# Eight slots for split weights, and norms that start token tile by token tile, in a two-block transformer kernel

## The reference

```python
def first_block(x, ...):                    # two layers
    # layer 0: differential attention (8 heads), layer 1: chunked attention with
    # a relative bias (16 heads); FFN of width 2816
    x = layer_norm(DEEPNORM_ALPHA * x + mix, ...)
    x = layer_norm(DEEPNORM_ALPHA * x + swiglu(x, w_in, w_out), ...)
...
def second_block(x, ...):
    z = rmsnorm(h, pre_mix_g) @ w_in        # then a gMLP and a gated linear attention mixer
    h = h + rmsnorm(concat(a, b) @ w_out, post_mix_g)
    f = rmsnorm(h, pre_ff_g) @ w_ff1
    h = h + rmsnorm(square(relu(f)) @ w_ff2, post_ff_g)
```

## Time and profile before

| | |
|---|---|
| runs | 1957.37, 1959.56, 1962.37 us; median 1959.56 |
| the profiled execution | 1956.62 us, span 1954.9 us, mean granted clock 0.978 |
| TensorE | 1843.4 us busy, 94%, 8392 matmuls |
| DVE, ACT, GpSimd | 938.2, 680.3 and 173.2 us busy |
| weight tiles | 309: 269 split by DVE, 40 by GpSimd |

### The profile page before, as it was taken

How to read it: one execution, slowest core, us unless ns; L and a number is a source line. 1 busy time by engine, 2 the same in 40 slices (tenths; PEclk the granted TensorE clock), 3 DMA queues, 4 the chain that set the end, 5 groups by cost and what they waited for, 6 DMA issues and landing times.

```text
span 1954.9 us, 21070 instructions
## 1 busy us (share of the span) xinstructions
PE 1843.4 (94%) x8392; PEld 1469.8 (75%) x8392; DVE 938.2 (48%) x1524; ACT 680.3 (35%) x1104; POOL 173.2 (9%) x108
## 2 busy tenths in 40 slices
PE   8998888999999899999799999996999879999998
PEld 7766667888888676666688888875877668888886
DVE  3688755333333824555633333357342654344344
ACT  3344432222223334554232222233445443323242
POOL 0322101000000500000200000013000240000000
PEclk9999999999999999999999999998999989999999
DMA  6322113333333432222133333343322333333231
GB/s 219 101 71 84 60 55 88 102 92 101 100 94 115 129 116 84 81 65 64 56 97 97 97 98 97 97 143 101 87 56 63 119 108 107 97 97 97 87 108 54
DMA packets 222744, 184.96 MB, mean 95 GB/s; under 512 B 9220, under 2 KB 178086, under 8 KB 222647
## 3 DMA queue, kind: packets, MB, share of 16 engines
q1 hardware_dynamic: 222646, 183.62, 30.9%
HBM read 181.45 MB, written 7.38 MB: 97 GB/s over the span
## 4 chain that ended last, share of the span: by engine, by line
PE 83%; DVE 13%; ACT 2%; issue 1%; POOL 0%; DMA 0%; SPq 0%; POOLq 0%; DVEq 0%; ACTq 0%
PE ps L472 25%; PE ps L473 24%; PE ps L474 24%; PE ps L759 2%; DVE x L1275 2%; DVE x L1280 2%; PE ps L769 1%; PE ps L719 1%; PE ps L781 1%; PE ps L658 1%; DVE stat L1367 1%; DVE arena L1305 1%; DVE xl L1196 1%; DVE wlo L1188 1%; DVE small L1263 1%
## 5 line engine op out<-in xcount | busy, mean ns | idle before, releaser
L1188 DVE TENSOR_TENSOR wlo<-raw,whi 128x1024 fp32r<-128x1024 f32 x269 | 330.2, 1229 | 489.6 <-ACT whi L924 487.8
L472 PE MATMUL ps<-xh,whi 128*128 128x512 f32 (+1 forms) x1416 | 547.9, 387 | 6.0 <-DVE xl L1196 6.0
L474 PE MATMUL ps<-xh,wlo 128*128 128x512 f32 (+1 forms) x1416 | 535.3, 378 | 0.0
L473 PE MATMUL ps<-xl,whi 128*128 128x512 f32 (+1 forms) x1416 | 535.1, 378 | 0.0
L924 ACT ACTIVATE whi<-raw 128x1024 fp32r<-128x1024 f32 x309 | 324.0, 1053 | 325.8 <-PE ps L474 323.9
L472 PE MATMUL ps<-whi,hh 128*128 128x512 f32 x800 | 319.7, 400 | 14.6 <-POOL wlo L1521 6.3
L472 PEld LDWEIGHTS ps<-xh,whi 128*128 128x128 f32 x1416 | 271.6, 192 | 58.2 <-DVE xl L1196 7.2
L473 PE MATMUL ps<-wlo,hh 128*128 128x512 f32 x800 | 315.0, 394 | 0.0
L474 PE MATMUL ps<-whi,hl 128*128 128x512 f32 x800 | 314.8, 393 | 0.0
L474 PEld LDWEIGHTS ps<-xh,wlo 128*128 128x128 f32 x1416 | 270.5, 191 | 49.0
L473 PEld LDWEIGHTS ps<-xl,whi 128*128 128x128 f32 x1416 | 271.0, 191 | 47.7 <-issue 2.9
(11 more groups left out here) (186 smaller groups left out, 1497.0 us busy)
## 6 DMA issues: line engine op xcount, KB each, us to landing
raw<-in_ffn_w_in SPq DMA_DIRECT2D x88, 512.0 KB, 3.8
raw<-in_w_ff SPq DMA_DIRECT2D x64, 512.0 KB, 3.9
raw<-in_ffn_w_out SPq DMA_DIRECT2D x56, 512.0 KB, 3.8
raw<-in_a_w_qkv SPq DMA_DIRECT2D x24, 512.0 KB, 5.1
raw<-in_w_in SPq DMA_DIRECT2D x20, 512.0 KB, 3.7
raw<-in_kv_w SPq DMA_DIRECT2D x16, 512.0 KB, 3.7
raw<-in_w_out SPq DMA_DIRECT2D x16, 512.0 KB, 3.8
bias_skewed<-bias_rows SPq DMA_DIRECT2D x8, 640.0 KB
```

Source lines behind the costliest of these rows:

```text
L472: e.matmul(o, ah, bh, start=start, stop=False)
L473: e.matmul(o, ah, bl, start=False, stop=False)
L474: return e.matmul(o, al, bh, start=False, stop=stop)
L1188: e.tensor_tensor(self.wlo[:, m % RING, :], self.raw[:, m % RING, :], f32(self.whi[:, m % RING, :]), ALU.subtract).then_inc(s.lo, 1)
```

## The change

- Split weights no longer lie in a ring of four but in slots: SPLIT = 6 always, and EXTRA = 2 more in the arena while attention and mixer don't need that room (`open_extra`, `close_extra`), so eight at every norm. `raw` stays a ring of four. DVE splits every tile.
- The last half ahead of a norm is one run over all its blocks (`runs = [blocks]`), token tile by token tile; `pairs` is gone. The transposes of tiles 0 and 1 stand inside tiles 2 and 3. FFN_GROUPS puts the group of six first, so that the last has four blocks.
- The step `feat` is TensorE's part alone; `xsplit` is that of ACT and DVE. The normalisation is a step `ln` of its own. `waiting` holds `pump` back from token tile 3 on.
- `projections` begins 4 (norms 1 to 3), 5 (norm 4) or 6 jobs (norm 5) on half the tokens, and attention B starts with it too: its values come behind the first four jobs, their second half inside `fill`, and AHEAD_B is 12.
- The mixer makes q0 and q1 within `projections` and interleaves its small steps with the value and gate products; four steps of the product with `w_out_2` (before: two) stand ahead of `squares(3)`. Several arena addresses move, `stat` shrinks, and 1024 bytes are reserved for dynamic DMA.

```diff
-RING = 4
-FFN_GROUPS = [(0, 8), (8, 8), (16, 6)]
+RAW = 4
+SPLIT = 6
+EXTRA = 2
+FFN_GROUPS = [(0, 6), (6, 8), (14, 8)]
 LN_EXP, SQRT, SILU = "natural_log_exp_and_others", "sqrt_and_others", "silu_and_others"
 
 AHEAD_A = 8
 ORDER_A = "- t3 - S0 S1 F0 w F1 - T0 S2 T1 S3 F2 - - - F3 n T2 -".split()
-AHEAD_B = 4
+AHEAD_B = 12
...
-    def pump(self):
-        while self.n_split < len(self.tiles) + RING - 1 and (
-                self.n_split < RING or self.n_split - RING in self.finished):
-            if self.on_pool:
-                self.pool_tiles[self.n_split] = len(self.pool_tiles)
+    def pump(self, most=2):
+
+        while most and self.slots and not self.waiting and self.n_split < len(self.tiles) + SPLIT + EXTRA:
+            slot, free = self.slots.pop(0)
+            self.slot_of.append(slot)
+            self.free_at.append(free)
+            if slot >= SPLIT:
+                self.extra_used[-1][slot] = self.n_split
             self.step("split", self.n_split)
             self.n_split += 1
+            most -= 1
 
     def take(self, *source):
         self.tiles.append(source)
         self.pump()
+        assert self.n_split >= len(self.tiles)
         return len(self.tiles) - 1
 
     def done(self, tile, sem, value):
         self.finished[tile] = (sem, value)
+        if self.slot_of[tile] < SPLIT or self.extra:
+            self.slots.append((self.slot_of[tile], (sem, value)))
         self.pump()
 
-    def settle(self):
-        while self.settling:
-            self.step(*self.settling.pop(0))
+    def open_extra(self, sem, value):
+
+        self.extra = True
+        self.extra_used.append({})
+        self.slots.extend((SPLIT + i, (sem, value)) for i in range(EXTRA))
+
+    def close_extra(self):
+        self.extra = False
+        self.slots = [x for x in self.slots if x[0] < SPLIT]
...
-    def projections(self, wanted, functions):
-        jobs = [self.job(*w) for w in wanted[:3]]
-        self.settle()
-        for job in jobs:
-            self.step("half", job, 0)
-        for norm, t in self.carry:
-            self.feat(norm, t)
-        self.carry = []
+    def projections(self, wanted, functions, norm, n):
+
+        jobs = []
+
+        def half(i):
+            if i < n:
+                jobs.append(self.job(*wanted[i]))
+                self.step("half", jobs[i], 0)
+
+        half(0)
+        if norm < 4:
+            self.feat(norm, 2)
+            self.xsplit(norm, 2)
+            self.step("ln", norm, 3)
+            half(1)
+            half(2)
+            self.feat(norm, 3)
+            self.xsplit(norm, 3)
+        else:
+            self.step("yscale", norm, 2)
+            self.step("ln", norm, 3)
+            self.waiting = False
+            self.pump(1)
+            half(1)
+            half(2)
+            self.feat(norm, 2)
+            self.xsplit(norm, 2)
+            self.step("yscale", norm, 3)
+            self.pump(1)
+            half(3)
+            half(4)
+            self.feat(norm, 3)
+            self.xsplit(norm, 3)
+        self.waiting = False
+        for i in range(len(jobs), n):
+            half(i)
...
+            ends = nh == 1 and norm is not None
+            if ends:
+                runs = [blocks]
+                self.step("table", SQRT)
+            elif nh == 1:
+                runs = [[k] for k in blocks[:-n]] + [blocks[-n:]]
...
+                    if ends and t == 3:
+                        self.waiting = True
...
+                        if ends and norm >= 4 and last and t == 3:
+                            self.feat(norm, 1)
+                            self.xsplit(norm, 1)
+                            self.step("ln", norm, 2)
...
+                        if ends and first and t == 3 and norm >= 4:
+                            self.feat(norm, 0)
+                            self.xsplit(norm, 0)
+                        elif ends and first and t >= 2 and norm < 4:
+                            self.feat(norm, t - 2)
+                            self.xsplit(norm, t - 2)
+                            if t == 3:
+                                self.step("ln", norm, 2)
...
+                            if ends and t < 2:
+                                if norm >= 4 and t == 1:
+                                    self.step("yscale", norm, 0)
+                                self.step("ln", norm, t)
+                            elif ends and t == 2 and norm >= 4:
+                                self.step("yscale", norm, 1)
...
+        self.open_extra("scores", 64)
...
+                self.projections(wanted, SILU, norm - 1, 4)
...
+        self.close_extra()
+        self.projections([(kind, p, w, c + p * 128) for p in range(2)
+                          for kind, w, c in (("q_b", "b_w_q", 0), ("k_b", "kv_w", 0))], LN_EXP, 2, 4)
         values = self.rows("v", ("kv_w", 1024), 0, 8, hh=False)
-        for i in range(32):
-            if i in (6, 9):
-                self.feat(*self.carry.pop(0))
-            if i == 9:
-                self.on_pool = False
-                self.step("table", LN_EXP)
+        out = self.rows("res", ("b_w_o", 0), 0, 8, norm=3)
+        for _ in range(16):
...
+            yield from proj(2)
+            yield from values
+            for p in range(3, 8):
...
+        out = self.rows("w", ("w_out_2", 0), 0, 8, k_first=4, norm=5)
+        for _ in range(4):
+            next(out)
...
-                    w.wait_ge(s.hi, m + 1)
-                    e.tensor_tensor(self.wlo[:, m % RING, :], self.raw[:, m % RING, :],
-                                    f32(self.whi[:, m % RING, :]), ALU.subtract).then_inc(s.lo_pool, 1)
-                    before = self.lo_at[m]
```

More of the change, by code:

```diff
@@ L150, in projections, with rows @@
             self.post(job)
-        for w in wanted[3:]:
+        for w in wanted[n:]:
             self.run(self.quarters(*w))
-    def rows(self, kind, source, row0, nk, k_first=0, ends=False, pairs=False, hh=True, norm=None, group=0):
-        later = []
+    def rows(self, kind, source, row0, nk, k_first=0, grouped=False, hh=True, norm=None, group=0):
         blocks = [(k_first + k) % nk for k in range(0, nk, 2)]
         n = min(3, len(blocks))
[L160 to L165, removed]
+        for nh in range(2):
+            ends = nh == 1 and norm is not None
[4 more added lines that the diff above has]
+                runs = [[k] for k in blocks[:-n]] + [blocks[-n:]]
+            elif grouped:
@@ L166, in rows @@
                 runs = [blocks[:n]] + [[k] for k in blocks[n:]]
             else:
-                runs = [[k] for k in blocks[:-n]] + [blocks[-n:]]
+                runs = [[k] for k in blocks]
             out, taken = {}, {}
             for run in runs:
[L171 to L174, removed]
+                for t in range(4):
+                    if ends and t == 3:
+                        self.waiting = True
@@ L247, in attention_a @@
         self.step("prepare_a")
-        out = self.rows("res", ("a_w_o", 0), 0, 8, ends=True, norm=1)
+        out = self.rows("res", ("a_w_o", 0), 0, 8, norm=1)
         def proj(h):
@@ L330, in fill @@
                 yield
-        self.step("bias", 0)
-        self.step("bias", 1)
-        self.run(proj(0))
         pieces = fill()
@@ L426, in mixer @@
         self.step("load_norm", 5)
-        out = self.rows("w", ("w_out_2", 0), 0, 8, k_first=4, ends=True, pairs=True, norm=5)
-        for h in range(4):
-            self.h[h] = 0
-        next(out)
-        next(out)
+        out = self.rows("w", ("w_out_2", 0), 0, 8, k_first=4, norm=5)
+        for _ in range(4):
+            next(out)
         self.squares(3)
@@ L479, in __init__ @@
     def __init__(self, new):
-        self.raw = [new(f"raw{i}") for i in range(RING)]
+        self.raw = [new(f"raw{i}") for i in range(RAW)]
         self.x = [new(f"x{i}") for i in range(4)]
@@ L665, in tensor @@
                 b = job.bank
-                wh, wl = self.weight(self.whi, job.tile, 8), self.weight(self.wlo, job.tile, 8)
+                wh, wl = self.weight(job.tile, 8)
                 if what == "half":
@@ L1005, in scalar @@
                     e.activation(self.mb[:, t, c], ps[b][:], ACT.Copy).then_inc(s.fb, 1)
-                if r.norm is not None and r.nh == 1:
-                    w.wait_ge(s.eps, 2)
-                    w.wait_ge(s.var, 4 * (r.norm - 1) + t + 1)
-                    e.activation(lsum[:, t:t + 1], mv[:, 2 * t + 1:2 * t + 2], ACT.Sqrt,
-                                 bias=eps6 if r.kind == "w" else eps5).then_inc(s.std, 1)
                 if r.kind == "f" and r.group == 3:
@@ L1021, in scalar @@
                                      scale=1.0 / D).then_inc(s.froot, 1)
+            elif what == "ln":
+                norm, t = arg
+                w.wait_ge(s.eps, 2)
+                w.wait_ge(s.var, 4 * (norm - 1) + t + 1)
+                e.activation(lsum[:, t:t + 1], mv[:, 2 * t + 1:2 * t + 2], ACT.Sqrt,
```

(1 more changed line is left out.)

234 lines of the change are left out of this document (118 added, 116 removed).

## The result

The changed kernel takes 1914.18 us (median of four runs, 1911.62 to 1916.28) against 1959.32 for the kernel before: the ratio is 0.9768, with a 95% interval of 0.975 to 0.9785. It is faster by 45 us. Forecast were 1873 and a range of 1860 to 1897, so the sign is right and half of the gain is missing: 41 us. The profiled execution took 1916.28 us, with a span of 1914.6.

What follows compares the result with a forecast made beforehand. TensorE bounds the kernel, busy 1843.4 of 1954.9 us; 93.2 us of idle and lost clock, less 1.4, 0.4, 3.6, 1.0 and 0.5, give 86.3 gained: 1959.56 - 86.3, forecast 1873 us, range 1860 to 1897.

Steps and rivals of the forecast that it cites:

- Six slots for four in attention A: Attention A: more split slots cost nothing; its 22.5 us of idle stay, give or take 3.
- the likeliest case: Whole kernel: the change works as forecast, 1873 us, own range 1860 to 1882; chance 0.63.
- The norms: Five norms: their 88.6 us of idle and lost clock go, except a 1.4 us stall at norm 4.
- handovers: Whole sum: 0.5 us taken for handovers not exactly as in the timeline.
- The signs named beforehand: No normalisation pass over 0.8 us, DVE split x289, transposes waiting under 3 us in all, clock 1.00 at every norm.
- the rival in which it stays low: Norms: the clock falls as now, 22.7 us stay lost, 1896 us; chance 0.05.
- The rival in which DVE becomes the bound: Norms: four splits in each chain, 24.6 us, and some 10 of clock, 1908 us; chance 0.07.
- Ahead of w_out_2: 1520 to 1540 us: with 24 matmuls instead of 12 on each side of `squares`, 4.6 us become 0.4.
- Attention B: Its start, values' second half under the first two pairs of heads with four banks held: 1 us lost.
- a sign of being wrong: Attention B: idle beyond 2 us in its first two pairs of heads would show the prediction wrong.
- The half jobs: Jobs run as two halves, 23 instead of 12: eleven times 0.33, 3.6 us added.
- the "in part" rival: Norms: small margins open a wait of 2 to 5 us at each, clock whole, 1883 to 1898; chance 0.2.

Runs made afterwards that it cites:

- e1: Changed kernel with split steps emitted at the take of the next weight tile, from attention A only: 1874.67 us, ratio 0.9571.
- e2: Kernel before with its pump bound RING instead of RING - 1, so splits stand where the changed kernel has them: 1989.43 us, ratio 1.0158.
- e6: Changed kernel with split steps at the take of the next tile throughout the whole network: 1868.48 us, ratio 0.954.
- e3: Kernel before with all splits on DVE and none on GpSimd, one line changed: 1920.95 us, ratio 0.9804.
- e9: e5 with `waiting` never set, so splits are not held back at a norm: 1880.06 us, ratio 0.9601.
- e5: Changed kernel with split steps at the take of the next tile in attention A and attention B: 1871.49 us, ratio 0.9556.
- e7: e5 with three half jobs at every norm, 15 jobs in halves for 23: 1891.45 us, ratio 0.9659.
- e4: Changed kernel with `done`, and so the split step, moved behind the job's own `post` step everywhere: 1885.56 us, ratio 0.9624.

## Why the prediction came out 41 us too low

**The step that failed** is one of those costed at nothing: "Six slots for four in attention A, whose TensorE waits for DVE's softmax and not for splits: its 22.5 us stay, give or take 3." They became 45.5, with 16.5 more of clock: 39.5 us. The observation in it was true, TensorE of the kernel before did not wait for splits, and it does not now. It waits for passes that stand behind a split. The prediction asked whether a split is late for its user; the question was what stands behind it in its queue, and it had asked just that of `waiting` at the norms. e1, e2 and e6 show it from three sides: the new kernel without the new place loses the cost, the old kernel with the new place gets it, and with the old place everywhere the changed kernel takes 1868.5, which is inside the likeliest case's own range of 1860 to 1882. No rival had this mechanism in attention A, so the range ended at 1897.

**The norms** were right. 88.6 us were to go but for 1.4; of norms 1 to 3 nothing is left. At norm 4 the idle time is 1.76 where the timeline gave 1.4, and its longest wait is the one worked out, for `xl` (1.6 us); 1.7 of clock come with it that I had not counted; norm 5 has 0.5, as much as the sum allowed for handovers. The four passes of a tile take 750 ns each, so that tile 0 is normalised 5.2 us after its residual add begins, for 5.3 worked out. The signs named beforehand are there: no pass over 0.76 us, 289 splits on DVE, and 0.2 us in all that the transposes wait for DVE. This is DVE's timeline of the changed kernel, norm 3:

```profile
955.63 0.69 DVE L1333 SCALAR_TENSOR_TENSOR x<-x,ps 128x512 f32<-128x512 f32 x1 [1.74 <-PE ps L528]
...
957.86 0.75 DVE L1390 SCALAR_TENSOR_TENSOR x<-x,small,arena 128x512 f32<-128x512 f32 x1
...
960.09 0.75 DVE L1395 SCALAR_TENSOR_TENSOR x<-x,small,arena 128x512 f32<-128x512 f32 x1
```

**The clock** stayed at 1.00 at norms 1 to 3 and 5, so the rival in which it stays low is out. What the prediction said against it, that the dips follow gaps of over 3 us, doesn't hold, though (last section). The Trainium skill (TensorE: Matmul & The Clock Gate, Part 4) says that transposes in TensorE's transpose mode don't count as busy in the same way for the clock. With groups of eight transposes among half jobs the clock fell at none of these four norms, so no consequence of that rule shows here.

**GpSimd's splits.** That they are what stretches the passes is shown by e3. The Trainium skill (SBUF — State Buffer, SBUF: two separate sides) calls the port pair that DVE and GpSimd share an exclusive lock, held for a whole instruction. The trace agrees: a pass of 0.75 us took 2.84 beside GpSimd's pair of splits, and in e3, without them, none was over 0.753. The rival in which DVE becomes the bound was priced by four splits in the chain at 5 us a norm; e9 shows 1.7 (8.6 by 5), and none at all in the changed kernel, whose holding back works.

**Ahead of w_out_2** 4.6 were to become 0.4 and are 3.6: 1.85 idle and 1.7 of clock. Moving the splits (e6) brings 0.3 and none, against 1.85 and none in e5, so the idle time was their place here too. The 1.7 of clock are absent in e5 already, where the place at w_out_2 is unchanged; why they came is open.

**Attention B** was given 1 us and lost 5.7 (9.4 for 3.7). In e5 and e6 it has 3.5 with the banks held as before, so the four held banks cost nothing, and the loss was the splits' place once more. The prediction had named idle in its first pairs of heads beyond 2 us as a sign of being wrong; they have 3.7 in 744 to 800.

**The half jobs** were to add 3.6. e7 confirms the price of one, yet TensorE's time without idle and clock is 1814.6 before and 1813.7 after. Something in the change gives the 3.6 back; I looked for no cause, and it stays open. In the sum it hides an error of 4 us in my favour.

**The sum.** Put together from the table, after against before: 85.7 gained at norms and w_out_2 (91.4 in the prediction), 0.9 by the rest of TensorE's time (3.6 lost), 5.7 lost in attention B (1), 39.5 in attention A (0), 2.9 of clock in the first 20 us, and 1.7 of clock gained in the mixer (not counted, either). With 0.2 more at the end that is 40 us, the difference of the spans being 40.3. The clock in the first 20 us was low in the profiled executions of the changed kernel, e1 and e3 (2.9 to 3.0), e2 and e5 (1.7 and 1.5), and not in those of before, e4 and e6 to e9, so it follows no edit that I can name.

**The chances.** Faster had 0.95. The forecast's own case held for every part but one place; the "in part" rival (1883 to 1898) named waits at the norms, of which norms 1 to 3 have none, and even its upper end is 16 us under the measurement.

## What to carry to other kernels

When slots or buffers are added, read where the list now puts the instruction that refills them, and not only how many there are: in a queue that runs in order, an instruction placed before its wait can be met holds all that stands behind it, and its engine's busy share can fall while TensorE waits more for it. Test it by comparing two waits before and after, refill for freeing event and the step behind for its engine; if both appear, emit the refill where the next tile is taken. And before restaging a norm, take GpSimd's elementwise work out from under DVE's passes: one line gave 37 us here, two fifths of what the whole change gives with its splits put back in place (91, e6).

## What the runs showed that I had not expected

- DVE was busy for 81% of attention A before (145.66 of 180 us) and for 72% after (125.97 of 176), and TensorE waited more for it. The busy share did not show the loss; what each engine waited for did.
- The clock fell after a gap shorter than the 3 us that the prediction took as the least: in the changed kernel TensorE idled for 2.47 us ahead of 124.93, and matmuls of 512 columns then took 0.63 us, 0.43 apart, from 125.98 until 128.97, for 0.39 and 0.23 before. TensorE's timeline:

```profile
124.93 0.52 PE L793 MATMUL ps<-ident,arena 128*128 128x128 f32 x3 [2.47 <-DVE arena L1289]
...
125.98 0.63 PE L526 MATMUL ps<-xh,whi 128*128 128x512 f32 x1
126.41 0.63 PE L527 MATMUL ps<-xl,whi 128*128 128x512 f32 x1
```

- A small wait can cost about as much again in clock, and doesn't always: in attention A 23.0 us more of idle came with 16.5 more of clock, and at norm 4 1.76 of idle with 1.7. But in e1 the same 1.76 us at norm 4 cost no clock (the row below), and the kernel before lost 1.7 in the mixer between 1441 and 1446 us with no idle near it. No rule that would have given the 16.5 in advance comes out of these runs.

```profile
1280.00:1330.00 50.00, 48.24 (x333) 44.47 (x332) 35.11 (x57) 19.19 (x34) 0.00 (x0) 1.00 0.22 70
```

- TensorE's time without idle and without the clock's loss is the same to 3 us in all eleven kernels (1812.5 in e7, 1813.7 to 1815.5 in the others), so that nearly every difference between them is a wait and what the clock makes of it.
